# Moving a norm's two small matmul groups from between two weight slabs into the second slab

## The reference

```python
def rms_norm(x, g):
    xf = x.astype(jnp.float32)
    y = xf * lax.rsqrt(jnp.mean(xf * xf, axis=-1, keepdims=True) + EPS)
    return (y * g.astype(jnp.float32)).astype(x.dtype)
...
        h = rms_norm(x, g_mix[l])
        z = h @ w_in[l]
...
        h = rms_norm(x, g_ffn[l])
        x = x + (jax.nn.silu(h @ w_gate[l]) * (h @ w_up[l])) @ w_down[l]
        gate = jax.nn.sigmoid(rms_norm(x, g_ple[l]) @ w_ple_gate[l])
        x = x + gate * (p[l].astype(x.dtype) @ w_ple_proj[l])
...
    h = _rmsnorm(x, g_pre_mix_2)
    proj = h @ w_in_2
...
    h2 = _rmsnorm(x, g_pre_ffn_2)
    x = x + _rmsnorm(_conv_gated_mlp(h2, w_up, conv_w, conv_b, w_down), g_post_ffn_2)
```

## Time and profile before

| | |
|---|---|
| median of 3 runs | 1812.79 us |
| lowest, highest | 1808.0, 1814.0 us |
| the profiled execution | 1802.71 us, its span 1801.4 us |
| TensorE (PE) busy | 1670.8 us, 93% |
| VectorE (DVE) busy | 901.8 us, 50% |
| ScalarE (ACT) busy | 619.1 us, 34% |
| mean granted TensorE clock | 0.962 of full speed |

### The profile page before, as it was taken

How to read it: one execution, slowest core, us unless ns; L and a number is a source line. 1 busy time by engine, 2 the same in 40 slices (tenths; PEclk the granted TensorE clock), 3 DMA queues, 4 the chain that set the end, 5 groups by cost and what they waited for, 6 DMA issues and landing times.

```text
span 1801.4 us, 18611 instructions
## 1 busy us (share of the span) xinstructions
PE 1670.8 (93%) x7851; PEld 1367.0 (76%) x7851; DVE 901.8 (50%) x1189; ACT 619.1 (34%) x769; POOL 11.7 (1%) x25
## 2 busy tenths in 40 slices
PE   6998968889999999999898989999999699999998
PEld 5788735567888888877787779878878488888886
DVE  5534467744444442236744544345443767777323
ACT  4215335433332222125542333323333444444311
POOL 1000000000000000000000000000000000000000
PEclk9999969899999999999999999999999799999999
DMA  4322200002233323232231112222332122222221
GB/s 145 94 88 71 71 6 1 1 18 88 83 103 106 95 94 106 94 111 76 88 96 51 47 53 94 94 94 73 106 102 70 47 94 94 94 94 94 106 94 70
DMA packets 122322, 144.28 MB, mean 80 GB/s; under 512 B 6009, under 2 KB 113872, under 8 KB 122240
## 3 DMA queue, kind: packets, MB, share of 16 engines
q1 hardware_dynamic: 120816, 139.87, 23.7%
q0 software_dynamic: 1232, 3.16, 0.6%
q10 hardware_dynamic: 192, 0.07, 0.0%
HBM read 140.99 MB, written 2.10 MB: 79 GB/s over the span
## 4 chain that ended last, share of the span: by engine, by line
PE 88%; DVE 6%; ACT 3%; issue 1%; DMA 1%; SPq 0%; DVEq 0%; ACTq 0%
PE bank L347 26%; PE bank L349 26%; PE bank L348 26%; PE bank L385 1%; PE bank L534 1%; PE bank L718 1%; PE bank L580 1%; PE bank L520 1%; PE bank L519 1%; PE bank L701 1%; PE bank L575 1%; DVE slab_lo L840 1%; DVE tmp L853 1%; DMA x_tm<-in_x 0%; PE bank L543 0%
## 5 line engine op out<-in xcount | busy, mean ns | idle before, releaser
L347 PE MATMUL bank<-h_hi,slab_hi 128*128 128x512 f32 x1384 | 552.0, 399 | 28.2 <-DVE h_lo L845 16.8
L348 PE MATMUL bank<-h_lo,slab_hi 128*128 128x512 f32 x1384 | 544.9, 394 | 0.0
L349 PE MATMUL bank<-h_hi,slab_lo 128*128 128x512 f32 x1384 | 544.7, 394 | 0.0
L840 DVE TENSOR_TENSOR slab_lo<-slab_raw,slab_hi 128x2048 fp32r<-128x2048 f32 x130 | 296.1, 2279 | 336.8 <-ACT slab_hi L1496 336.5
L347 PEld LDWEIGHTS bank<-h_hi,slab_hi 128*128 128x128 f32 x1384 | 264.3, 191 | 90.6 <-issue 29.6
L1496 ACT ACTIVATE slab_hi<-slab_raw 128x2048 fp32r<-128x2048 f32 x130 | 246.3, 1896 | 214.3 <-DMA slab_raw<-in_w_down 142.6
L348 PEld LDWEIGHTS bank<-h_lo,slab_hi 128*128 128x128 f32 x1384 | 264.5, 191 | 57.0 <-issue 2.2
L349 PEld LDWEIGHTS bank<-h_hi,slab_lo 128*128 128x128 f32 x1384 | 263.7, 191 | 55.8
L879 DVE TENSOR_TENSOR tmp<-bank,x_rstd_rows 128x512 f32<-128x512 f32 x98 | 67.3, 689 | 110.4 <-PE bank L349 110.3
L347 PE MATMUL bank<-slab_hi,h_hi 128*128 128x256 f32 x320 | 90.8, 284 | 2.2 <-DVE slab_lo L840 2.2
L348 PE MATMUL bank<-slab_lo,h_hi 128*128 128x256 f32 x320 | 90.6, 283 | 0.0
(11 more groups left out here) (352 smaller groups left out, 1860.1 us busy)
## 6 DMA issues: line engine op xcount, KB each, us to landing
slab_raw<-in_w_in SPq DMA_DIRECT2D x40, 1024.0 KB, 4.9
slab_raw<-in_w_up SPq DMA_DIRECT2D x33, 1024.0 KB, 4.9
slab_raw<-in_w_down SPq DMA_DIRECT2D x22, 1024.0 KB, 4.9
slab_raw<-in_w_gate SPq DMA_DIRECT2D x11, 1024.0 KB, 5.2
slab_raw<-in_w_o SPq DMA_DIRECT2D x4, 1024.0 KB, 4.9
slab_raw<-in_w_ple_gate SPq DMA_DIRECT2D x4, 1024.0 KB, 4.9
slab_raw<-in_w_ret_o SPq DMA_DIRECT2D x4, 1024.0 KB, 5.1
slab_raw<-in_w_sgu_o SPq DMA_DIRECT2D x4, 1024.0 KB, 5.1
```

The lines of the kernel that those rows point to most:

```text
L347: T.matmul(ps, a_hi, b_hi, start=start, stop=False, skip_group_check=skip)
L348: T.matmul(ps, a_hi, b_lo, start=False, stop=False, skip_group_check=skip)
L349: return T.matmul(ps, a_lo, b_hi, start=False, stop=stop, skip_group_check=skip)
L840: V.tensor_tensor(w_lo[j][:, 0:n], raw[j][:, 0:n], w_hi[j][:, 0:n].bitcast(F32), ALU.subtract).then_inc(slab_lo, 1)
```

## The change

The two halves of TensorE's `norm_rows` become `norm_sum` (the sums of squares) and `norm_spread` (the row). `slab_fm` takes a norm's number and issues the first after 4 of its 16 steps (12 of 48 large matmuls) and the second after 8 (24 of 48). The call moves from between the first and the second slab into the second slab, for all five norms. No other engine's program is changed.

```diff
-        def slab_fm(g, names, src_hi=h_hi, src_lo=h_lo, ready=None):
+        def slab_fm(g, names, src_hi=h_hi, src_lo=h_lo, ready=None, norm=None):
+
 
             T.wait_ge(slab_lo, g + 1)
...
             for n in range(2 * KT):
                 k, t = (n // 2, n % 2) if ready else (n % KT, n // KT)
+                if norm is not None and n == KT // 2:
+                    norm_sum(norm)
+                if norm is not None and n == KT:
+                    norm_spread(norm)
                 if ready and t == 0:
                     T.wait_ge(ready[k][0], ready[k][1])
...
-        def norm_rows(i):
+        def norm_sum(i):
             T.wait_ge(squares_summed, i + 1)
             ps = take(("sum", i), rot())
             whole(("sum", i), sum_rows(ps[:, 0:TT], tmp[0], True, True, True))
+
+        def norm_spread(i):
             T.wait_ge(norm_diag, i + 1)
             ps = take(("row", i), rot())
             whole(("row", i), T.matmul(ps[:, :], ones, tmp[1], start=True, stop=True))
...
         slab_fm(0, [("c", 0), ("c", 1)], ready=h_ready(0))
-        norm_rows(0)
-        slab_fm(1, [("c", 2), ("c", 3)])
+        slab_fm(1, [("c", 2), ("c", 3)], norm=0)
...
             slab_fm(FF + 2 * n, [("gate", 2 * n), ("gate", 2 * n + 1)], ready=h_ready(1) if n == 0 else None)
-            if n == 0:
-                norm_rows(1)
-            slab_fm(FF + 2 * n + 1, [("up", 2 * n), ("up", 2 * n + 1)])
+            slab_fm(FF + 2 * n + 1, [("up", 2 * n), ("up", 2 * n + 1)], norm=1 if n == 0 else None)
...
-            slab_fm(PLE + 1 + n, [("pg", 2 * n), ("pg", 2 * n + 1)], ready=h_ready(2) if n == 0 else None)
-            if n == 0:
-                norm_rows(2)
+            slab_fm(PLE + 1 + n, [("pg", 2 * n), ("pg", 2 * n + 1)], ready=h_ready(2) if n == 0 else None,
+                    norm=2 if n == 1 else None)
...
-            slab_fm(IN2 + n, [("rot", 2 * n), ("rot", 2 * n + 1)], ready=h_ready(3) if n == 0 else None)
-            if n == 0:
-                norm_rows(3)
+            slab_fm(IN2 + n, [("rot", 2 * n), ("rot", 2 * n + 1)], ready=h_ready(3) if n == 0 else None,
+                    norm=3 if n == 1 else None)
...
             slab_fm(UP2 + 2 * n, [("a2", 2 * n), ("a2", 2 * n + 1)], ready=h_ready(5) if n == 0 else None)
-            if n == 0:
-                norm_rows(4)
-            slab_fm(UP2 + 2 * n + 1, [("b2up", 2 * n), ("b2up", 2 * n + 1)])
+            slab_fm(UP2 + 2 * n + 1, [("b2up", 2 * n), ("b2up", 2 * n + 1)], norm=4 if n == 0 else None)
```

## The result

The changed kernel takes 1824.55 us (median of 7 runs, 1816.5 to 1832.25) against 1811.39 us before (7 runs, 1804.19 to 1816.35). The ratio is 1.0076, with a 95% interval of 1.0048 to 1.0105: slower by 0.8%. A ratio is estimated from all the runs of both kernels, so it need not be that of the two medians. The profiled execution has a span of 1823.2 us, 21.8 more than that of before.

What follows compares the result with a forecast made beforehand. The prediction took TensorE, busy 93% of the span, to bound the kernel. Third-slab shifts of +7.2 us and clock losses of +4.8 gave +12.0 on the median of 1812.79: 1824.8 us, range 1812 to 1831.

Steps and rivals of the forecast that it cites:

- path and clock: Norms 2, 3, 4: later third slabs, +2.2, +1.4, +4.1 us, and a low-clock stretch behind their waits, +1.6 each.
- TensorE after the change: Second slab: row starts 6.39 us after slab start, slab could end at 13.03; sums and row cost what they did.
- The 0.16 us at each of the two groups: Sums and row in a stream: possible saving per group, at most 1.6 us over five norms, forecast then some 1823.
- The path behind the row: Row's start to third slab's low part: 4.31, 7.97, 10.09, 9.36, 11.04 us at norms 0 to 4, against 6.64 of work.
- the three places of the earlier trace: TensorE's waits for a sum of squares before the change: 10.5 us over three places, one said to be another norm's.
- The ends of slabs: Second slab's end was taken as SyncE's next load issue, 842.56 at norm 2 before the change.
- The second slab at norm 2: Its low part was taken as ready at the slab's start, as at norms 0 and 3; no wait there.
- What is late next: the clock: Third slabs' idle times bring low-clock stretches: 1.6 us each at norms 2, 3 and 4, none at norm 1; +4.8 us.
- the 2.0 ahead of norm 4's row: Norm 4's second slab: low clock after TensorE resumes puts the row off by 2.0 us, included in its +4.1.
- That the clock holds: Rival: third slabs late, but no new low-clock stretch follows; +5.2 to +7.2 us, 1818 to 1820; chance 0.22.
- That the path is hidden: Rival: third slab's low part ready within 6.64 us of the row; -4.7 us, 1808; chance 0.08.
- Nothing to measure: Rival: third slabs late, clock holds, sums nearly free in the stream; 0 to +5 us, 1813 to 1818; chance 0.15.

Runs made afterwards that it cites:

- second profiles: The changed kernel and the kernel before, each run and profiled once more with nothing changed; 1821.16 and 1814.59 us.
- the split ahead: Changed kernel, with VectorE and ScalarE making the third slab's high and low parts before the norm's root or reciprocal; 1809.35 us, ratio 0.999 to before.
- norms 1 to 4 alone: Changed kernel with norm 0 put back between its slabs, so only norms 1 to 4 are moved; 1820.12 us, ratio 1.0043 to before.
- the fill: Changed kernel plus thrown-away matmuls in TensorE's two waits at norm 4, 20 before the second slab, 16 before the third; 1807.05 us in one run.
- the first experiment: Only norm 0 moved into its second slab, norms 1 to 4 left as in the kernel before; 1812.57 us against 1809.93, ratio 1.0002.
- the third and fourth experiments: Third: the split ahead, 1809.35 us, ratio 0.999. Fourth: the early row, ratios 0.9992 and 0.9953.
- with the fill too: The early row plus 13 thrown-away matmuls in TensorE's wait ahead of norm 4's sums; 1807.27 us, ratio 0.9966 to before.
- the early row: Changed kernel with sums issued ahead of the second slab and row after 2 of its 16 steps; 1809.2 and 1803.75 us, ratios 0.9992 and 0.9953.

## Why the prediction was right

The forecast was 1824.8, a sum of +12.0 on the median then known, 1812.79; measured is 1824.55 against 1811.39, +13.2 with an interval of 8.7 to 19. The mechanism is the forecast one: the third slabs wait for their low parts. That the two times lie 0.25 us apart is luck, since the terms for the clock were wrong at every norm that had one. The parts, between the first and between the second profiles:

| | forecast | first profiles | second profiles |
|---|---|---|---|
| norm 0 | -1.3 | -1.4 | -1.4 |
| norm 1 | +0.8 | +1.3 | +1.3 |
| norm 2, path and clock | +2.2, +1.6 | +1.8 | +0.2 |
| norm 3, path and clock | +1.4, +1.6 | +1.9 | +0.8 |
| norm 4, path and clock | +4.1, +1.6 | +7.6 | +7.8 |
| sum | +12.0 | +11.2 | +8.6 |

*TensorE after the change.* Sums to row took 3.66 to 3.68 us at all five norms, as worked out (0.95 + 2.72). At norm 2 the row starts at 846.69, and SyncE's next issue is at 853.23: 6.54 us against 6.64. So the row is 0.1 us cheaper in the stream, and the sums not at all. The 0.16 us at each of the two groups, estimated from the Trainium skill, page "TensorE: Matmul & The Clock Gate", section "Single matmul latency", which gives its formula for a bf16 matmul (these are float32), is not borne out: 0.1 a norm in place of 0.3.

*The path behind the row.* Shown. It was 4.21, 7.87, 9.98, 9.25 and 10.92 us at norms 0 to 4 from the row's start to the low part, 0.1 under the forecast; the waits are 1.42, 3.53, 2.81 and 4.47 against 1.33, 3.45, 2.72 and 4.40. Two experiments moved it and the time followed: the split ahead took the waits away, and a row 2.72 us later made them 2.7 us longer. Of the three places of the earlier trace rows two belong to norms that the change leaves alone (1.48 and 5.74 us), not one; the sum does not use them.

*The ends of slabs.* I read them from SyncE's issue, which comes 0.19 us behind TensorE's last matmul (446.98 in the earlier trace rows against an issue at 447.17, say). Where a wait replaces this end, the forecast is 0.2 us short: part of the 0.5 at norm 1. The other 0.3 us there is not accounted for.

*The second slab at norm 2.* It waited 0.66 us for its own low part, which I had only for norms 1 and 4. In the first profile of before this norm's first slab ran its start at half clock (0.53 in the earlier trace rows); after the change it did not in either profile, TensorE was done sooner, and met the split. So the stretch grew by 1.8 us and not by the path's 2.2. In the profile with norms 1 to 4 alone, where the low stretch was there, it grew by 2.4. Against the second profile of before it grew by 0.2 only.

*What is late next: the clock.* This step was wrong in its sizes, and its errors partly cancel: 4.8 us and the 2.0 ahead of norm 4's row were charged, 5.1 found, and in other places. At norms 2 and 3 I charged 1.6 us each for a low stretch behind idle times of 3.45 and 2.72 us. None came, in four profiles out of four (the change twice, norms 1 to 4 alone, and the fill, which left these two norms as in the change). At norm 4 I charged 2.0 ahead of the row and 1.6 behind the wait. The 12 matmuls ahead of the sums ran at half clock (8.89 us from the slab's start to the row against 6.39: 2.5), and the third slab had 5.5 us of it, 2.6 us lost. The fill showed this sum: 5.1 us. The prediction also took it that an idle time of 1.29 us leaves the clock at 1.00. It read that at norm 1; at norms 2 and 3 the same wait was followed by half clock in one profile of before and in the first experiment. Whether that wait brings it on was not tested; the four profiles that have norms 2 and 3 moved show no low stretch in the second slab. What the change costs at these two norms so depends on the profile of before: +0.2 to +1.8 us at norm 2, -1.3 to +1.9 at norm 3.

*Rivals.* That the clock holds was right for norms 2 and 3 and wrong for norm 4. That the path is hidden is what the third and fourth experiments made true, and the norms' stretches were then shorter; in the runs the gain shows in one set of the fourth alone. The change itself never had it. "Nothing to measure" needed the sums to be nearly free in the stream, and they took 0.95 us as before.

*The runs' scatter.* The profiled pair differs by 21.8 us and the medians by 13.2, against 11.2 or 8.6 at the norms. The profiled excess is in attention, and the change can't be blamed for it: one and the same kernel showed 414.5 and 421.8 us there, another 431.8 and 414.5, with granted clocks of 0.91, 0.89, 0.87 and 0.90. The kernel with the fill, which has the whole change in it, took 414.3. The medians exceed the norms' sum by 2.0 or 4.6 us; 11.2 lies inside the interval, 8.6 at its lower edge, and no run shows where the rest would be.

## What to carry to other kernels

A wait that is filled with other work is only won if nothing hangs on what the wait ends in. Before moving a step later, measure the path behind its result to the next thing that the bounding engine needs, and compare it with the work that stays behind the step, not with the gap. Here the row had to stay where it was in time; only the six matmuls that fit into the gap could go ahead of it. That version beat the kernel before in one set of runs (0.9953) and equalled it in the other (0.9992), and was faster with the fill too (0.9966); in both it is faster than the change (1.0076).

Where runs scatter by more than the effect, compare stretches between waits that recur in every profile, and take more than one profile of each kernel. Two profiles of the early row agreed to 0.1 us at the norms while their spans differed by 17.6; two of the kernel before differed by 1.6 us at norm 2, where the clock fell once more in one of them. What such a comparison can be trusted for shows only when both kernels are profiled again.

## What was not expected of the hardware

TensorE's granted clock did not go by the length of an idle time alone. The third slabs' waits of norms 2 and 3 (3.53 and 2.81 us in the changed kernel) left it at 1.00 in all four profiles that have them; a row still later made the third slabs' waits 4.13, 6.25 and 5.52 us at norms 1 to 3, and each was followed by 0.56 or less. The wait of 3.72 us at norm 3's first slab (868.01 in the earlier trace rows) came with half clock in all thirteen profiles. The one of 2.17 us at norm 2's (815.64) came with it in six, both of before among them, and not in seven, both of the change among them; the profile with norms 1 to 4 alone, whose norm 2 is that of the change, had it, so the change does not decide it. And the wait of only 1.29 us ahead of the row was followed by half clock in one of two profiles of before at norm 2. What tells these places apart was not tried.
